# Adding the gathered expert rows by matrix products with a diagonal of routing weights, in a two-layer NSA/MLA decoder trunk with a mixture of experts

## The reference, cut to what matters

```python
for i in range(DEPTH):                                  # 2 layers
    h = rmsnorm(x, norm_mix[i])
    x = x + (nsa_mixer(h, ...) if i % 2 == 0 else mla_mixer(h, ...))
    h = rmsnorm(x, norm_ffn[i])
    x = x + hier_moe(h, ...)

def hier_moe(x2, ...):                                  # x2: 512 x 1024
    weights = g_w * top_p / sum(top_p)                  # 512 x 2, one weight per token and choice
    ...
    ys = (silu(xb @ w_gate[e]) * (xb @ w_up[e])) @ w_down[e]
    out[token] += slot_w[:, None] * ys                  # two rows of ys per token
```

## Time and profile before

| | us |
|---|---|
| median of 3 runs | 1709.32 |
| lowest and highest run | 1707.04, 1713.43 |
| the profiled execution, whole | 1703.69 |
| its span, first to last instruction | 1700.7 |
| PE busy | 1462.1 |
| DVE busy | 612.1 |
| ACT busy | 332.4 |
| POOL busy | 252.1 |

### The profile page before, as it was taken

One profiled execution on the slowest core, in us unless ns is written; L12 is line 12 of the kernel. 1 busy time (PEld: TensorE's weight loads), 2 busy tenths in 40 slices (PEclk: granted clock), 3 DMA queues, 4 the chain that ended last, 5 costly groups with the idle time before them and its releaser, 6 DMA issues.

```text
span 1700.7 us, 24539 instructions
## 1 busy us (share of the span) xinstructions
PE 1462.1 (86%) x9187; PEld 926.3 (54%) x9187; DVE 612.1 (36%) x1520; ACT 332.4 (20%) x966; POOL 252.1 (15%) x296
## 2 busy tenths in 40 slices
PE   7999999999899777777777799999998777777776
PEld 3655466555666555545454455655865545455553
DVE  3145677743522221222214537523522222212125
ACT  2122377741210000000000235512100000000000
POOL 1121100000211111111113224000211111111112
PEclk9999999999999999999999899999999999999998
DMA  5214110042699999999998200451999999999996
GB/s 231 69 50 173 75 76 1 2 176 109 254 427 427 428 429 428 429 429 428 427 428 337 112 1 1 174 235 62 351 425 428 428 429 429 428 428 429 428 426 228
DMA packets 41280, 479.28 MB, mean 282 GB/s; under 512 B 11798, under 2 KB 12326, under 8 KB 23360
## 3 DMA queue, kind: packets, MB, share of 16 engines
q1 hardware_dynamic: 24688, 447.34, 62.4%
q0 software_dynamic: 15232, 26.35, 4.5%
q10 hardware_dynamic: 1296, 4.72, 0.8%
HBM read 460.01 MB, written 47.19 MB: 298 GB/s over the span
## 4 chain that ended last, share of the span: by engine, by line
PE 51%; DMA 39%; DVE 5%; issue 1%; ACT 1%; POOL 0%; DVEq 0%; SPq 0%; POOLq 0%; ACTq 0%
DMA sb_ring<-moe_w 26%; DMA sb_rows_space<-moe_w 10%; PE ps L1104 9%; PE ps L1292 7%; PE ps L1501 6%; PE ps L1113 5%; PE ps L1607 2%; PE ps L1637 2%; PE ps L1622 2%; PE ps L1334 2%; PE ps L1472 2%; PE ps L1365 2%; PE ps L1361 1%; PE ps L1445 1%; PE ps L1535 1%
## 5 line engine op out<-in xcount | busy, mean ns | idle before, releaser
L1104 PE MATMUL ps<-sb_ring,sb_x_block 128*64 128x256 f32 x2816 | 327.8, 386 | 83.1 <-DMA sb_ring<-moe_w 80.4
L1104 PEld LDWEIGHTS ps<-sb_ring,sb_x_block 128*64 128x64 f32 x2816 | 287.3, 198 | 160.4 <-issue 87.1
L714 POOL DMA_INDIRECT expert_rows<-sb_y_sb,sb_row_now x124 | 134.2, 1083 | 777.3 <-DVE sb_y_sb L1896 748.6
L1895 DVE COPY sb_row_now<-sb_row_of 128x1 uint32 (+1 forms) x124 | 19.0, 154 | 637.1 <-PE ps L1113 614.5
L1113 PE MATMUL ps<-sb_ring,sb_hidT 128*64 128x512 f32 x704 | 173.1, 613 | 29.8 <-ACT sb_hidT L817 29.8
L817 ACT COPY sb_hidT<-ps 128x128 f32<-128x128 f32 x128 | 33.9, 265 | 815.2 <-PE ps L1179 815.2
L1104 PE MATMUL ps<-sb_rows_space,sb_x_block 128*64 128x256 f32 x1280 | 148.5, 384 | 44.4 <-DMA sb_rows_space<-moe_w 44.4
L1104 PEld LDWEIGHTS ps<-sb_rows_space,sb_x_block 128*64 128x64 f32 x1280 | 132.3, 198 | 78.8 <-issue 60.3
L1292 PE MATMUL ps<-sb_xsT,sb_rows_space 128*128 128x512 f32 x256 | 114.7, 594 | 2.1 <-DVE sb_rows_space L2122 1.3
L1900 DVE TENSOR_TENSOR sb_x_block<-sb_xsT,sb_moe_gain 128x512 f32<-128x512 f32 x128 | 88.6, 692 | 25.2 <-issue 20.9
L1113 PEld LDWEIGHTS ps<-sb_ring,sb_hidT 128*64 128x64 f32 x704 | 43.0, 137 | 97.2 <-issue 50.9
(11 more groups left out here) (306 smaller groups left out, 1677.5 us busy)
## 6 DMA issues: line engine op xcount, KB each, us to landing
sb_ring<-moe_w SPq DMA_DIRECT2D x88, 3072.0 KB, 31.6
sb_rows_space<-moe_w SPq DMA_DIRECT2D x40, 3072.0 KB, 31.6
sb_xsT<-nsa_w_group SPq DMA_DIRECT2D x2, 2048.0 KB, 14.0
sb_ring<-nsa_w_group SPq DMA_DIRECT2D x2, 2048.0 KB, 8.0
sb_xsT<-nsa_w_out SPq DMA_DIRECT2D x1, 4096.0 KB, 12.5
kept_rows<-sb_rows_space SPq DMA_DIRECT2D x8, 512.0 KB, 2.6
token_rows<-sb_rows_space ACTq DMA_DIRECT2D x8, 512.0 KB, 2.6
sb_rows_space<-kept_rows SPq DMA_DIRECT2D x8, 512.0 KB, 26.9
```

Of the source, the lines that this page charges most:

```text
L714: pool.indirect_dma_start(out=ys_dram.rearrange("r (j n) -> (r j) n", j=2), out_offset=bass.IndirectOffsetOnAxis(ap=row_now[:, u:u + 1], a ...
L1104: last = nc.tensor.matmul(ps[j * BLOCK:(j + 1) * BLOCK, bank, 0:2 * P].rearrange("p (g n) -> p g n", g=2), x_rows[:, :, k], weights[:, 0:2 ...
```

## The change

DVE writes a tile `scaled_ident` of eight 128 x 128 blocks, once per layer: block `c` is the identity with each diagonal element multiplied by `sent_wt[:, c]`. PE multiplies the gathered rows `y_at(c)` by block `c` and accumulates into the banks that already hold `kept_sums` of the tile (`sent_sums(t)`): two choices times two halves of 512 columns, four products of 128 x 128 by 128 x 512 per tile. `add_rows` is gone; `add_kept` adds the whole expert output of the tile in one pass. In layer 0 DVE's copy `turned_half(0)` moves behind the addition of tile 3.

```diff
+        scaled_ident, _ = cut(scratch, 0, TOPK * TILES, P)
...
                                                 start=(u == 0), stop=False)
+                def sent_sums(t):
+                    if t == 0:
+                        pe.wait_ge(scaled_ident_ready, l + 1)
+                    for k in range(TOPK):
+                        c = k * TILES + t
+                        pe.wait_ge(rows_landed[c], 32 * l + 32)
+                        for j in range(2):
+                            last = nc.tensor.matmul(ps[:, kept_bank(t) + j, :], scaled_ident[:, c, :],
+                                                    y_at(c)[:, j * 512:(j + 1) * 512], start=False, stop=(k == TOPK - 1))
+                    last.then_inc(kept_done, 1)
...
                 kept_sums(0, 1)
                 kept_sums(1, 1)
+                sent_sums(0)
+                sent_sums(1)
                 for t in range(2, TILES):
                     for u in range(2):
                         kept_sums(t, u)
+                    sent_sums(t)
...
                 join_hidden(0)
+                step(nc.vector.tensor_tensor(scaled_ident, ident[:, :].unsqueeze(1).to_broadcast([P, TOPK * TILES, P]),
+                                             sent_wt[:, :].unsqueeze(2).to_broadcast([P, TOPK * TILES, P]), ALU.mult))
+                step.join()
+                nc.vector.engine_nop().then_inc(scaled_ident_ready, 1)
                 if l == 0:
                     mla_tables()
                 keep_here(0)
...
-                def add_rows(t, k):
-                    c = k * TILES + t
-                    dve.wait_ge(rows_landed[c], 32 * l + 32)
-                    if k == 0:
-                        dve.wait_ge(x_loaded[t], 16 * (l + 2))
-                    step(nc.vector.scalar_tensor_tensor(out=x[:, t, :], in0=y_at(c), scalar=sent_wt[:, c:c + 1],
-                                                        in1=x[:, t, :], op0=ALU.mult, op1=ALU.add))
...
                     dve.wait_ge(kept_done, l * TILES + t + 1)
+                    dve.wait_ge(x_loaded[t], 16 * (l + 2))
...
-                add_rows(0, 0)
                 dve.wait_ge(silu_done, base + SENT + 2)
                 join_hidden(1)
-                add_rows(1, 0)
                 keep_here(1)
-                add_rows(0, 1)
                 add_kept(0)
-                add_rows(1, 1)
                 add_kept(1)
...
                 scale(n, 0)
-                add_rows(2, 0)
-                turned_half(m, 0)
-                add_rows(2, 1)
                 add_kept(2)
                 scale(n, 1)
-                add_rows(3, 0)
-                add_rows(3, 1)
                 add_kept(3)
+                turned_half(m, 0)
                 turned_half(m, 1)
```

More of the change, by code:

```diff
@@ L377, in build @@
         y_kept = sem("y_kept")
+        scaled_ident_ready = sem("scaled_ident_ready")
         rows_filled = sem("rows_filled")
@@ L1254, in kept_sums @@
                         last = nc.tensor.matmul(ps[:, kept_bank(t) + j, :], shares_T[rows, u, t * P:(t + 1) * P], y_sb[rows, u, :],
-                                                start=(u == 0), stop=(u == 1))
-                    if u == 1:
-                        last.then_inc(kept_done, 1)
+                                                start=(u == 0), stop=False)
+                def sent_sums(t):
[8 more added lines that the diff above has]
+                    last.then_inc(kept_done, 1)
                 n = SENT
@@ L2005, in moe_dve @@
                     for t in range(2, TILES):
-                        add_rows(t, 0)
-                        add_rows(t, 1)
                         add_kept(t)
```

## The result

| us | before | after |
|---|---|---|
| median of 9 runs each | 1709.22 | 1712.11 |
| lowest and highest run | 1705.85, 1713.43 | 1710.84, 1713.84 |
| the profiled execution, whole | 1703.69 | 1711.92 |
| its span | 1700.7 | 1710.1 |

The ratio of after to before is 1.0018, with a 95% interval of 1.0009 to 1.0026: some 3.1 us slower (1.5 to 4.4), which is within the 0.5% and inside the range of 1704 to 1717. The spans of the two profiled executions lie 9.4 us apart, much more than that, so the first thing to settle is where in the traces those 9.4 us are. The profiled execution of before, 1703.69, is also shorter than every one of the 9 runs in this table (lowest 1705.85).

A forecast was written before the change was run, and what follows sets the result against it. PE was taken as busy for 86% of the span, with DVE bounding the layer ends and PE after the change. Layer 0's -3.4 and layer 1's +3.9 gave +0.5 us; forecast 1710, range 1704 to 1717.

The forecast's parts named there:

- DVE no longer holds the join: Both layer ends: expert 63's join waits for ACT alone; layer 1's kept products start at 1681.0 instead of 1684.23 us.
- The price of a product: New float32 products on PE: 0.43 us a record, 0.86 a product, 13.8 for sixteen in a layer.
- third rival: Products are cheap, a quarter of the price: layer 1 gains 6.2 us, whole near 1695; chance 0.02.
- PE becomes the bound: Both layer ends: PE, not DVE, decides when a tile is whole; DVE idles before each add_kept.
- PE's row of 19.0 us: Each layer's end: twelve kept products (5.2 us) and sixteen new ones (13.8) run on end on PE.
- Layer 1, +3.9: End of layer 1: last tile done at 1701.5 instead of 1697.64 us, a cost of 3.9.
- Layer 0, -3.4: End of layer 0: latents(0) starts 2.5 us earlier and loses its slow part, 0.9; gain 3.4.
- slow part: Layer 0's latents(0): 7.97 us at a clock of 0.69 becomes 7.03 at full clock, 0.9 gained.
- The sum: Whole kernel: -3.4 in layer 0 and +3.9 in layer 1 make +0.5 us, forecast 1710.
- First rival: PE's clock falls as before in both layer ends, losing 5 and 3.5 us: +9, 1719; chance 0.08.
- Second rival: Layer 0's gain isn't kept, as something in or before MLA is late: +3.9, 1713; chance 0.14.
- Fourth rival: Layer 0 gives more as a clock phase in MLA falls better: -3 to -6 net, 1705; chance 0.04.

The follow-up runs named there:

- e6: The change in layer 1 alone, as e2, with both factors of the new products read as bfloat16; 1703.99 us, ratio 0.9971 to the kernel before.
- e8: The kernel before, unchanged, profiled a second time; it ran at 1706.26 us.
- e1: The change in layer 0 alone, layer 1 as in the kernel before; 1708.26 us, ratio 0.9995 to the kernel before.
- e2: The change in layer 1 alone, layer 0 as in the kernel before; 1712.94 us, ratio 1.0025 to the kernel before.
- e5: The kernel before with only the join of expert 63 moved ahead of add_rows(0, 0), both layers; 1709.29 us, ratio 0.9999.
- e3: The kernel before, no new products, DVE reordered: join and kept-row copy earlier, each tile finished before the next; 1705.39 us, ratio 0.9977.
- e7: As e3, with DVE's copy of turned tile 0 three steps later in layer 0; 1701.42 us, ratio 0.9958 to the kernel before.

## Why the prediction was right, and which of its terms were not

The forecast was 1710, +0.5 us by its sum, and the kernel came out at 1712.11, +3.1 (1.5 to 4.4). The verdict, no change that matters, and both mechanisms are right: a loss in layer 1 by PE's row, a gain in layer 0. The size isn't quite: +0.5 lies below the measured interval. That the time fell well inside a range of 13 us proves little by itself, since the range also held two rivals (1713 and 1705), and a gain and a loss of like size nearly cancel. By its steps:

- **DVE no longer holds the join.** Right: 0.03 us behind ACT in both layers, and kept products start 5.34 us after K1 (1685.67 - 1680.33), against 5.34 in the forecast (1681.0 - 1675.66).
- **The price of a product.** Right: records 0.43 us apart, as read from MLA; e6 confirms that this price decides layer 1. The third rival, cheap products, is out; with products really made cheap, e6's layer 1 gained 5.1 us, where that rival had 6.2.
- **PE becomes the bound.** Right: DVE waited 25.1 us for it, over both layers.
- **PE's row of 19.0 us.** Mis-sized, and this is the term that failed: it counted the products as one even stream and put the changes between kept and gathered ones at nothing. With run-out the forecast had 19.3 us for the 28 products, the trace has 1705.81 - 1685.67 = 20.14. Each group is right inside, but each change of kind costs: from the start of four kept products to the next group it is 1687.59 - 1685.67 = 1.92 instead of 1.72, eight sent ones take 1694.65 - 1687.59 = 7.06 instead of 6.88, four 1700.20 - 1696.57 = 3.63 instead of 3.44. That is some 0.19 us at each of the five changes, 0.9 in all. At each, the weight load after the change has idle time of 0.76 before it, where loads inside a group have 0.24 (both in the rows of layer 0 above).
- **Layer 1, +3.9.** Measured +4.8 between the two traces to the last addition, of which the changes of kind are 0.9. To the end it is +4.7, and +5.3 against the mean of three traces.
- **Layer 0, -3.4.** Measured -2.5 between the two traces: the same 0.9 us of changes puts the start of `latents(0)` at 27.45 instead of 950.1 - 923.52 = 26.6 after K0. Its slow part is gone, as forecast (7.10 for 7.97). Against the mean of four traces it is -2.0.
- **The sum.** With the changes of kind it becomes +0.5 + 2 x 0.9 = +2.3, inside the measured interval; the two traces give +4.7 - 2.5 = +2.2. Against the means it is +5.26 - 2.01 = +3.2: the one profiled before was slower than its like in just these two places (39.54 against 39.06, 25.04 against 24.52), which is no more than its like stray by.
- **First rival, the clock falls.** Out: 1.00 in every stretch from 924 to 964 and from 1678 to 1708, those shown above and the others. (Its price of +9 on 1709.3 is 1718, not 1719.) What the forecast took for granted, that the clock of before falls in layer 1, isn't so in each execution: e8 kept 1.00 there.
- **Second rival, layer 0's gain is lost, 1713.** The time alone would fit (+3.9 against 1.5 to 4.4). The landmarks speak against it: -2.0 in layer 0, and the stretch behind it in after and e1 (717.75, 718.25) no longer than in e8 and e2 (718.45, 717.57). The runs by themselves don't decide it.
- **Fourth rival, more in layer 0.** Not seen with this change.

What the forecast didn't see is how much lay in the order. It explained the whole idle time by the join, where e5 shows that the join is only the first of two steps that stand behind a wait, and e3 and e7 show that the order alone gains 3.9 and 7.2 us without any product.

## What to carry to other kernels

When a change takes work off one engine and also moves its steps, run the new order with the old work: here the order was the gain, and the work moved was a loss. Where an engine goes through its list in order, as DVE does here, look at every step that another engine waits for and that stands behind a wait for a transfer, not just at the one that the profile names: moving the join alone gained nothing. Share a sum such that both engines finish together rather than hand it over whole. Price a row of products by kind and by the changes between kinds, and judge a difference of a few microseconds at landmarks close to the change, since two traces of one kernel differ by as much elsewhere.

## What the runs showed of the hardware

- A change between products that use 64 rows of the array (the kept ones) and products that use all 128 costs some 0.19 us over the stream of 0.43 a record, seen at all five changes in both layers of after. No wait in PE's list explains it: ahead of `kept_sums(2, 0)` there is none, and the load has 0.76 us all the same; between the two choices of a tile there is one, and the loads keep their 0.24.
- A product of 128 x 128 by 128 x 512 takes 0.86 to 0.88 us in float32 (after, e2) and at most 0.23 in bf16 in the same place (e6).
- The granted clock isn't fixed by the program: with the same code and the same wait of PE for the join in layer 1 (2.25 and 2.23 us) it was 0.50 in 1682 to 1688 in before and 1.00 in 1680 to 1698 in e8.
- At the start of layer 1's experts, 16 turns of a gathered chunk are drawn out over some 5 us in nine of ten traces, with gaps of 0.2 to 1.1 us for which the profile names no releaser but the issue (in e5 the first one, 0.20 us, has the transfer of the tokens). In all nine the granted clock falls to 0.50 behind the gaps, and the products after them take 5.10 to 5.83 us where the profiled before, at 1.00, has 3.74. The stretch around it was 712.6 us in the one trace without the gaps and 717.6 to 719.9 in the others; up to the first of these products it is 246.3 against 251.2 to 252.6. What causes them stays open: no run aimed at it.
